# Hybrid mLSTM and attention block on one core: h tiles ahead of splits, attention and mLSTM scores from split operands, and the feed-forward norm's token scale moved to gate and value

## What is computed

```python
h = rmsnorm(x, g_pre_mix)
proj = h @ w_in                              # q, k, v, gates of mLSTM, q, k, v of attention, merge gates
# attention, 8 heads, two maps of 128 channels each, 256 value channels
s = einsum(q, k) * scale - slope * dist ; p = softmax(s) ; attn = p[0] - lam * p[1] ; attn @ v
# mLSTM, 8 heads of 256 channels: q, k = silu(causal_conv4(.)), then (q @ k) * w @ v / max(...)
mix = (g_m * (hm @ w_branch_m) + g_a * (ha @ w_branch_a)) @ w_out
x = x + rmsnorm(mix, g_post_mix)
h = rmsnorm(x, g_pre_ffn)
u = causal_conv3(h @ w_up) ; gate, val = split(u)
x = x + rmsnorm((gelu(gate) * val) @ w_down, g_post_ffn)
```

## Time and profile before

| what | value |
|---|---|
| median of 3 runs | 1849.39 us (1849.22 to 1849.85) |
| the profiled execution | 1849.28 us, span 1847.5 us, mean granted clock 0.999 |
| PE busy | 1837.0 us (99%) |
| DVE busy | 1148.7 us (62%) |
| ACT busy | 891.9 us (48%) |
| POOL busy | 68.3 us (4%) |
| DMA | 351.44 MB, 190 GB/s |

### The profile page before, as it was taken

The page is one execution under the profiler, slowest core; times in us unless marked ns, Lnnn a source line. Parts: engine busy times, 40 slices in busy tenths (PEclk is TensorE's granted clock), DMA queues, the critical chain, the costliest instruction groups (busy, mean ns, idle before and its releaser), DMA issues.

```text
span 1847.5 us, 35631 instructions
## 1 busy us (share of the span) xinstructions
PE 1837.0 (99%) x13860; PEld 1745.6 (94%) x13860; DVE 1148.7 (62%) x1372; ACT 891.9 (48%) x1172; POOL 68.3 (4%) x92
## 2 busy tenths in 40 slices
PE   9999999999999999999999999999999999999998
PEld 9999999999999999999999889999999999988886
DVE  5766566656665576555555558666667667755555
ACT  6554445444544445444434446555555555544443
POOL 1820000000000000000000000000000000000000
PEclk9999999999999999999999999999999999999999
DMA  7575665666656655665666755666666666665554
GB/s 258 171 204 174 195 180 173 183 186 180 182 172 191 181 177 173 191 194 193 186 198 196 261 187 157 194 190 196 192 194 193 190 195 186 199 217 193 193 192 142
DMA packets 164369, 351.44 MB, mean 190 GB/s; under 512 B 10920, under 2 KB 11456, under 8 KB 163648
## 3 DMA queue, kind: packets, MB, share of 16 engines
q1 hardware_dynamic: 162640, 344.11, 60.6%
q10 hardware_dynamic: 1280, 5.08, 0.7%
q0 software_dynamic: 368, 1.09, 0.3%
HBM read 348.12 MB, written 2.12 MB: 190 GB/s over the span
## 4 chain that ended last, share of the span: by engine, by line
PE 97%; DVE 1%; DMA 1%; issue 1%; ACT 0%; POOL 0%; DVEq 0%; POOLq 0%; ACTq 0%
PE ps L1467 26%; PE ps L1468 26%; PE ps L1469 26%; PE ps L1740 11%; PE ps L1744 6%; PE ps L1700 1%; DMA raw<-in_w_in 0%; PE ps L1548 0%; PE ps L1676 0%; DMA raw<-in_w_out 0%; ACT w_hi L634 0%; PE ps L1557 0%; DVE w_lo L1005 0%; PE ps L1677 0%; PE ps L1505 0%
## 5 line engine op out<-in xcount | busy, mean ns | idle before, releaser
L1005 DVE TENSOR_TENSOR w_lo<-raw,w_hi 128x1024 fp32r<-128x1024 f32 x637 | 777.9, 1228 | 611.4 <-ACT w_hi L634 610.6
L634 ACT ACTIVATE w_hi<-raw 128x1024 fp32r<-128x1024 f32 (+1 forms) x641 | 674.9, 1059 | 739.8 <-PE ps L1469 580.2
L1467 PE MATMUL ps<-h,w_hi 128*128 128x256 f32 x3180 | 880.3, 277 | 1.0 <-DVE h L1001 0.9
L1469 PE MATMUL ps<-h,w_lo 128*128 128x256 f32 x3180 | 878.8, 276 | 0.0
L1468 PE MATMUL ps<-h,w_hi 128*128 128x256 f32 x3180 | 878.8, 276 | 0.0
L1467 PEld LDWEIGHTS ps<-h,w_hi 128*128 128x128 f32 x3180 | 597.1, 188 | 1.7 <-DVE w_lo L1005 1.1
L1468 PEld LDWEIGHTS ps<-h,w_hi 128*128 128x128 f32 x3180 | 597.1, 188 | 0.3
L1469 PEld LDWEIGHTS ps<-h,w_lo 128*128 128x128 f32 x3180 | 597.1, 188 | 0.0
L1740 PE MATMUL ps<-w_hi,ks_hi 128*128 128x512 f32 x448 | 174.5, 389 | 0.0
L1744 PE MATMUL ps<-w_lo,ks_hi 128*128 128x512 f32 x448 | 174.4, 389 | 0.0
L1740 PE MATMUL ps<-w_hi,ks_lo 128*128 128x512 f32 x448 | 138.1, 389 | 0.0
(11 more groups left out here) (204 smaller groups left out, 1486.9 us busy)
## 6 DMA issues: line engine op xcount, KB each, us to landing
raw<-in_w_in SPq DMA_DIRECT2D x287, 512.0 KB, 3.7
raw<-in_w_up SPq DMA_DIRECT2D x176, 512.0 KB, 4.4
raw<-in_w_down SPq DMA_DIRECT2D x88, 512.0 KB, 4.6
raw<-in_w_branch_m SPq DMA_DIRECT2D x32, 512.0 KB, 4.5
raw<-in_w_branch_a SPq DMA_DIRECT2D x32, 512.0 KB, 4.5
raw<-in_w_out SPq DMA_DIRECT2D x32, 512.0 KB, 4.7
x<-in_x ACTq DMA_DIRECT2D x1, 2048.0 KB, 12.2
gm<-in_channel_rows SPq DMA_DIRECT2D x3, 512.0 KB, 7.4
```

Of the source, the lines that this page charges most:

```text
L634: return nc.scalar.activation(out_ap, in_ap, ACT.Copy, scale=scale)
L1005: nc.vector.tensor_tensor(w_lo[:, at:at + UNIT], raw[:, slot, :], w_hi[:, at:at + UNIT].bitcast(F32), ALU.subtract).then_inc(lo_done, 1)
L1467: nc.tensor.matmul(out_ap, stat_hi, mov_hi, start=start, stop=False, skip_group_check=True)
L1469: return nc.tensor.matmul(out_ap, stat_lo, mov_hi, start=False, stop=stop, skip_group_check=True)
```

## The change

Five things are done.

1. In the first mixing turn the h tiles 8 to 15 are made one step earlier, ahead of that step's split (tiles 8 and 9 at step 1).
2. The attention scores' 256-column products and the mLSTM scores' first half use split operands. The halves lie in parts of `hm_hi`, `hm_lo`, `ha_hi`, `ha_lo` that aren't used yet, and in a new `m_k0`. ACT copies (steps 12, 16, 36, 44) and DVE subtracts (steps 13, 16, 37, 45). The attention's scores are behind unit 18 in place of 17; maxima, exponentials and normalization are one step later each; the transposes stay behind unit 25.
3. `x1` is transposed without the scaling by token; `xn` isn't made there. The residual comes in smaller pieces (`X1_PIECES`), the first four up units are written out by halves (`first_up_unit`), and the bank of the first tile changes.
4. The squares of `x1`'s second token block and both sums are made in the first up turn; the scale by token goes through DRAM to a row on all partitions (`up_row`).
5. In each up turn DVE multiplies gate (step 8) and value (step 0 of the next turn) by that row, from PSUM into `raw_up`; bias term and taps read `raw_up`. Some steps of the up turn are one later.

```diff
+X1_PIECES = ((0, 0, HALF), (0, HALF, HALF), (1, 0, T), (1, T, T)) + tuple((1, c, HALF // 2) for c in range(HALF // 2, D, HALF // 2))
...
@@ gpsimd
             for b in range(TB):
                 inverse_root(b, S_MS + PIECES_OF[b][0], mix_sum, b + 1, S_RS, mix_rs)
+            for b in range(TB):
                 inverse_root(b, X_MS + ROW_PIECES_OF[b][0], x_sum, TB + b + 1, X_RS, x_rs)
+            pool.wait_ge(x_rs, 2 * TB)
...
+                pool.dma_start(scales_dram.rearrange("(b p) -> p b", p=P), stat[:, X_RS:X_RS + TB]).then_inc(up_scale_out, 16)
+            pool.wait_ge(up_scale_out, 16)
+            pool.dma_start(up_row, scales_dram.partition_broadcast(P)).then_inc(up_scales, 16)
@@ scalar, mix_turn
+                    if first and 1 <= u < 5:
+                        early_tile(2 * u + 6)
+                        early_tile(2 * u + 7)
                     if u or not first:
                         split_ahead(g, U_MIX, BASE_MIX, u, home_mix)
-                    if first and 2 <= u < 6:
-                        early_tile(2 * u + 4)
-                        early_tile(2 * u + 5)
...
+                    if u in (12, 16):
+                        scalar.wait_ge(read_qk, g * 2 + (1 if u == 12 else 2))
+                        copy(lam[:, 3:4], (qT if u == 12 else kT)[:, 0, 0:1])
+                        if u == 12:
+                            ins = copy(hm_hi[:, ds(g * 4, 4), 0:P], qT[:, :, P:T])
+                        else:
+                            ins = copy(ha_hi[:, ds(g * 4, 4), :], kT[:])
+                        ins.then_inc(qk_hi, 1)
...
-                    if u in (20, 22):
-                        j = (u - 20) // 2
+                    if u in (21, 23):
+                        j = (u - 21) // 2
                         scalar.wait_ge(a_max, g * 2 + (j + 1))
...
+                    if u == 36:
+                        scalar.wait_ge(qk_ready, g * 2 + 1)
+                        copy(lam[:, 3:4], qT[:, 0, 0:1])
+                        copy(hm_hi[:, ds(g * 4, 4), :], qT[:]).then_inc(mq_hi, 1)
+                    if u == 44:
+                        scalar.wait_ge(qk_ready, g * 2 + 2)
+                        copy(m_k0[:, 0, :, :], kT[:, :, 0:P]).then_inc(mk_hi, 1)
@@ scalar, first up turn
-            for i in ROW_PIECES_OF[1]:
-                residual_squares(i)
-            norm_tiles(KT, C_GPF, {10: lambda: first_up_split(3)})
+            norm_tiles(KT, C_GPF, {8: lambda: first_up_split(3)})
...
+                    if first and 1 <= u <= 4:
+                        residual_squares(u + 1)
@@ vector, mix_turn (the early tiles as on scalar)
+                    if u == 37:
+                        vec.wait_ge(mq_hi, g + 1)
+                        nc.vector.tensor_tensor(hm_lo[:, ds(g * 4, 4), :], qT[:], hm_hi[:, ds(g * 4, 4), :].bitcast(F32),
+                                                ALU.subtract).then_inc(m_lo, 1)
+                    if u == 45:
+                        vec.wait_ge(mk_hi, g + 1)
+                        nc.vector.tensor_tensor(m_k0[:, 1, :, :], kT[:, :, 0:P], m_k0[:, 0, :, :].bitcast(F32),
+                                                ALU.subtract).then_inc(m_lo, 1)
...
-                    if u in (21, 23):
-                        j = (u - 21) // 2
+                    if u in (22, 24):
+                        j = (u - 22) // 2
                         vec.wait_ge(a_exp, g * 2 + (j + 1))
@@ vector, first up turn
-            residual(1, 0, x1, x1_ready)
...
-            normed(1, xn, x1, TB, (TILE_0, Q0_REST, Q1))
...
+            residual(1, 0, x1, x1_ready, X1_PIECES[:5])
+
+            norm_tiles(KT, C_GPF, {2: lambda: split(BASE_UP + 1, 1, away(1)),
+                                   4: lambda: residual(1, 0, x1, x1_ready, X1_PIECES[5:]),
+                                   6: lambda: split(BASE_UP + 2, 2, away(2)), 10: lambda: split(BASE_UP + 3, 3, away(3))})
...
+                vec.wait_ge(pe_done, g * U_UP + units_done(BASE_UP + U_UP - 1))
+                nc.vector.tensor_tensor(raw_up, tiles_of(1), up_tiles, ALU.mult).then_inc(val_copied, 1)
...
+                    if first and u == 5:
+                        mean_square(ROW_PIECES_OF[0], X_MS, x_ms, 4, x_sum)
+                        mean_square(ROW_PIECES_OF[1], X_MS, x_ms, 4, x_sum)
...
+                    if u == 8:
+                        vec.wait_ge(pe_done, g * U_UP + units_done(BASE_UP + 7))
+                        if first:
+                            vec.wait_ge(up_scales, 16)
+                        nc.vector.tensor_tensor(raw_up, tiles_of(0), up_tiles, ALU.mult).then_inc(gate_copied, 1)
@@ tensor
-                    if u == 17:
-                        pe.wait_ge(read_qk, g * 2 + 2)
+                    if u == 18:
+                        pe.wait_ge(qk_lo, g * 2 + 2)
...
-                                nc.tensor.matmul(ps[:, bank, P:P + T], q[:, P:T], k[:, 0:T], start=True, stop=True)
+                                t = 4 * g + 2 * j + m
...
+                                three(ps[:, bank, P:P + T], hm_hi[:, t, 0:P], hm_lo[:, t, 0:P], ha_hi[:, t, :], ha_lo[:, t, :],
+                                      start=True, stop=True)
...
                     if u == 46:
                         pe.wait_ge(qk_ready, g * 2 + 2)
+                        pe.wait_ge(m_lo, g * 2 + 2)
                         pe.wait_ge(a_done, g + 1)
...
-            again(xn, 34, 4)
...
+            again(6, 8)
```

More of the change, by code:

```diff
@@ new lines, in _ @@
+            pe.wait_ge(gained, 3)
+            for k in range(2, 6):
+                tile(k, 0)
+            pe.wait_ge(gained, 4)
+            for k in range(6, 8):
+                tile(k, 0)
+            again(6, 8)
+            pe.wait_ge(gained, 5)
+            pe.wait_ge(x1_ready, 2)
+            for k in range(8, 10):
+                tile(k, 0)
+            pe.wait_ge(x1_ready, 3)
+            for k in range(0, 2):
+                tile(k, 1)
+            pe.wait_ge(x1_ready, 4)
+            for k in range(2, 4):
+                tile(k, 1)
@@ new lines, in first_up_unit, with place, products @@
+            def first_up_unit(u):
+                def place(kk, t):
+                    c = away(u) + kk * 512 + t * P
+                    return ps[:, t // 2, t % 2 * T:t % 2 * T + T], 2 * u + kk, slice(c, c + P)
+                def products(kk, weights, tiles, start=False):
+                    for t in range(4):
+                        out_ap, k, c = place(kk, t)
+                        last = nc.tensor.matmul(out_ap, weights[:, c], tiles[:, k, :], start=start and t % 2 == 0, stop=False,
+                                                skip_group_check=True)
+                    return last
+                if u == 0:
+                    ready(BASE_UP)
+                    pe.wait_ge(h_hi_done, 10)
+                    products(0, w_hi, h_hi, True)
+                    products(0, w_lo, h_hi)
+                    pe.wait_ge(x1_ready, 5)
+                    for k in range(4, 8):
+                        tile(k, 1)
+                    pe.wait_ge(h_done, KT + 1)
+                    products(0, w_hi, h_lo)
+                    pe.wait_ge(h_done, KT + 2)
+                    products(1, w_hi, h_hi)
+                    products(1, w_hi, h_lo)
+                    products(1, w_lo, h_hi).then_inc(pe_done, 1)
+                    return
+                pe.wait_ge(hi_done, BASE_UP + u + 1)
+                for kk in range(2):
+                    pe.wait_ge(h_done, KT + 2 * u + kk + 1)
+                    products(kk, w_hi, h_hi)
+                    products(kk, w_hi, h_lo)
+                ready(BASE_UP + u)
+                products(0, w_lo, h_hi)
+                products(1, w_lo, h_hi).then_inc(pe_done, 1)
@@ new lines, in late_tiles @@
+            def late_tiles(u):
+                if u == 2:
+                    pe.wait_ge(x1_ready, 6)
+                    for k in range(8, 10):
+                        tile(k, 1)
+                    pe.wait_ge(h_done, KT + 1)
+                    for k in range(10, 12):
+                        tile(k, 0)
+                        tile(k, 1)
+                if u == 3:
+                    pe.wait_ge(x1_ready, 7)
+                    pe.wait_ge(h_done, KT + 4)
+                    for k in range(12, 16):
+                        tile(k, 0)
+                        tile(k, 1)
```

198 lines of the change are left out of this document (89 added, 109 removed).

## The result

The changed kernel takes **1868.2 us** (median of 4, 1866.5 to 1870.7), beside 1849.3 for the kernel before on the same chip: a ratio of 1.0104, 95% interval 1.0086 to 1.0121. The forecast was 1859.5, range 1852 to 1865. The direction was right and so were most of the mechanisms; the time lies outside the range.

The account below looks back on a forecast made before the run. The prediction took TensorE (PE), busy 99% of the span, to bound the kernel. Start, scores, passage, mixing-turn waits and token scale summed as 1849.3 - 1.0 - 2.9 - 3.5 + 17.6 + 0 = 1859.5 us, range 1852 to 1865.

Parts of the forecast that it names:

- Start: Before unit 4 of the first mixing turn: earlier h tiles remove PE's idle 0.86 us and part of the refill, 1.0 us less.
- Scores: Attention and mLSTM scores: eight 256-column products a turn as split products save 0.09 us each, 2.9 us in four turns.
- Softmax: Before the attention probability transposes: exponentials now stand behind the copy of v, so PE waits 1.6 us more a turn.
- Unit 45: In each mixing turn: the wait for q and its copy delay DVE's row, so PE waits 1.35 us for this unit's split.
- mLSTM scores: In each mixing turn: the same delay makes k's low half late, so PE waits 1.5 us more before these scores.
- rival (a): Mixing turns: the waits hide, as ACT's and DVE's steps keep enough distance; only gains are left, 1842 us; chance 0.09.
- Passage: Into the up phase: PE transposes x1 itself instead of running dummy transposes, so unit 4 starts 3.5 us earlier.
- The token scale: Up turns: DVE's added multiplications stay hidden, and the scale's two DMAs, 3 us each, land in time; cost 0.
- rival (c): First up turn: the scale lands late and adds 2 to 8 us, giving 1862 to 1868 us; chance 0.08.
- rival (d): PE's clock falls to half for one unit after each of twelve waits, costing 33 us, giving 1892 us; chance 0.04.

Follow-up runs that it names:

- s2_q_later: The changed kernel with q's high half copied at ACT's step 38, not 36, and its low half subtracted at DVE's step 39, not 37: 1863.06 us.
- s3_scale_pe: The changed kernel with the row of token scales made on the chip by DVE, PE and ACT, without the two DMAs through DRAM: 1861.05 us.
- s11_scores_alone: The kernel before with the split scores alone, in the change's order; start tiles and feed-forward side as before: 1865.12 us, ratio 1.0091.
- s8_more_dmas: s4_all_four with two rounds of three small DMAs by GpSimd at the up phase's start and two at the end: 1876.08 us, one execution.
- the first four experiments: Single edits to the changed kernel: second head's exponentials earlier (1861.95 us), q's halves later (1863.06), k's low half earlier (1864.11), scale row without DRAM (1861.05).
- s9_unused_pair: s4_all_four with the change's scattered store and broadcast load issued by GpSimd, and nothing waiting for them: 1841.81 us.
- s4_all_four: The changed kernel with exponentials earlier, q's halves later, k's low half earlier and the scale row made without DRAM: 1842.37 us, ratio 0.9963.

## Why the prediction was off, step by step

- **Start** (-1.0 forecast): -0.85, as reasoned.
- **Scores** (-2.9): -2.2. The mLSTM and attention places gave 0.56 us a turn, not 0.72. The bound from below (2.0), which allowed for changing between the forms, was the nearer one.
- **Softmax** (+1.6 a turn): 1.42 in three turns, 2.16 in the first. The chain was right link by link: copy of v, exponentials, two splits, normalization. In the first turn POOL is busy with the gates, and two of DVE's one-input multiplications take 1.01 us together where they take 0.54 later, a small one before them 0.45 for 0.23; with 0.79 for 0.75 in the last step these make up the 0.74 us:

```profile
88.56 1.01 DVE L1238 TENSOR_SCALAR prob<-prob,sm 128x128 f32<-128x128 f32 x2
```

- **Unit 45** (+1.35 a turn): 1.0 in three turns, none in the first. I took the second turn for all four. In the first the conv taps run in one row of six without the 0.17 us that the others lose between pairs, so it is 11.0 us from k's scaling to that split and not 11.5; and the scaling starts 12.1 us ahead of PE's need and not 11.6. Each makes half of the difference. The split is done at 146.1, just when PE comes.

```profile
138.38 2.78 DVE L1037 SCALAR_TENSOR_TENSOR kT<-prob,chan,kT 128x255 f32<-128x255 f32 x6
...
328.31 0.87 DVE L1037 SCALAR_TENSOR_TENSOR kT<-prob,chan,kT 128x255 f32<-128x255 f32 x2
329.35 0.88 DVE L1037 SCALAR_TENSOR_TENSOR kT<-prob,chan,kT 128x254 f32<-128x254 f32 x2 [0.17 <-issue]
```

- **mLSTM scores** (+1.5 a turn): 1.19. The last low half came at 343.3 in the second turn; 339.8 plus the 3.8 us by which that turn was later makes 343.6.
- Together the three were 17.6 by forecast, and are 14.1 of waiting and 2.3 beyond it, 16.4. That the sum comes so near is in part luck: the waits were forecast 3.5 too long, and what each costs beyond its idle time wasn't in the forecast. Of rival (a), that they hide, nothing is left.
- **Passage** (-3.5): -4.5, near the bound of 4.6. The forecast had PE wait 1.1 us at unit 4 for its low half. It doesn't: the up units that are written out by halves are the first eight, and not four as the list of changes says, and from the second on each begins with its 16 products from `w_hi`, and the low half, split from 1140.92 to 1142.15, is wanted at 1143.09:

```profile
1141.28 1.98 PE L1842 MATMUL ps<-h,w_hi 128*128 128x256 f32 x16
1143.09 1.07 PE L1842 MATMUL ps<-h,w_lo 128*128 128x256 f32 x8
```

- **The token scale** (0): +8.9, **the step that failed**. Its timing was otherwise right: the sums were to be done 8.4 us after unit 4 starts (1129.2 to 1137.6), and POOL had both scales 8.5 after (1141.28 to 1149.77); PE was to be late from a landing 15.8 after unit 4, and was from 16.3 (1164.56 - 6.95 = 1157.6). Wrong was the landing, 3 us taken for each DMA "near the short end as these two move little". They took 8.3 and 5.8. The rows for it were in the profile before: the earlier trace rows is a mixture: stores of whole rows are its 1.9 to 2.2, the broadcast load is 5.9, and the four loads of single numbers by token are 6.2 to 7.9. Split by tile, the row behind the stores and the load of `neg_g`, and that behind the loads of `um`, in the kernel before:

```profile
DMA to landing us min/median/max: 2.2/4.0/5.9
...
DMA to landing us min/median/max: 6.2/7.0/7.9
```

No store of single numbers stands in that trace; by the rows of the nearest form, loads of single numbers and the broadcast, the sum is 12 to 14 us, so a landing past the threshold and a wait of 5 to 6 us (8.4 + 12.1 to 13.8, less 15.8): rival (c) was the likeliest case and had a chance of 0.08. The Trainium skill (DMA: Bandwidth & Descriptors, Anatomy of one DMA) has 2.0 us fixed and little more for 1 KB; the runs agree for a store in one piece (1.6 to 3.1) and contradict it for the scattered one (8.1 to 10.0 in all profiles). The same page's opening table says that under 512 B the engines read, modify and write; that speaks against this store, and I had left it out. It doesn't explain the price by itself, as the pairs are under 512 B too and took 3.3.
- **The clock** (rival (d), 0.04): half right. It did not fall behind any of the waits of 1.0 to 1.4 us. It fell in all five profiles with the 7 to 8 us at unit 12, where 20 to 28 products ran at the slow pitch, 2.0 to 2.7 us each time (2.7 was forecast), and behind the 2.15 us of the first turn in three profiles of the six that have that wait (s2_q_later, s3_scale_pe, s11_scores_alone; not in the profile after), there for 10 to 16 products, 1.5 to 1.6 us; and behind the 2.65 us of s8_more_dmas. What decides it at such lengths stays open. It may be why the times of the changed kernels with the 2.15 us wait spread over 1.9 to 5.5 us and those of the others over 0.9 to 2.4; but the kernel before, which has no such wait, spread over 2.95 us in the eight executions beside the first four experiments.

Without the misjudged landing the other terms, as measured, give 1849.3 + 8.9 = 1858.2: the path through the mixing turns was read well, and one number decided.

## What to carry to other kernels

Cost a small DMA by rows of the same form (single numbers, whole rows, broadcast), never by its bytes, and split a min/median/max by tile before taking an end of it. When a step is added to engines that run in a hand-written order, its place matters more than its length: the same splits cost 14 us of waits in one order and none in another. And a mechanism that repeats by turns is checked in the first turn apart, where other engines are busy and loops not yet begun.

## What the runs showed of the hardware

- A store of 256 single fp32 numbers to DRAM took 8.1 to 10.0 us, of 128 pairs 3.3 to 5.3, of the same kilobyte in one piece 1.6 to 3.1. While such a store was under way in s9_unused_pair, the weight loads ran at 52 GB/s for 6 us, where s4_all_four has 249.
- PE's granted clock fell to 0.50 behind a wait of 2.15 us in three of six profiles, behind 2.65 us in the one that has it, with 6.95 to 8.0 us in all five, and not behind 2.92 us that followed 5.4 us of dummy transposes. A fall cost 1.5 to 2.7 us.
- A wait cost PE some 0.2 us beyond its idle time as the profile counts it.
- A pair of DVE's one-input multiplications (128 and 256 columns) took 1.01 us with POOL busy and 0.54 without; a pair of two-input ones 0.79 and 0.75.
